# Attention and output projection of the first 128 tokens in another order

## The chip, the cores and the metric

The program runs on one NeuronCore of one Trainium2 chip. The metric is the device time of one execution in microseconds. TensorE (PE) does matmuls, PEld is its weight loading, VectorE (DVE), ScalarE (ACT) and GpSimd (POOL) do elementwise work, and SyncE (SP) issues most DMAs. Each engine runs its own instructions in order, and semaphores order the engines against each other.

## The reference

Two transformer blocks run over 256 tokens of 1024 features, in float32. Cut to what matters here, the first block is:

```python
qa, ka, va, pb, qm = split(rms_norm(x) @ w_in)
out_a = sliding_window_attention(qa, ka, va)   # 6 heads, window 128, query blocks of 128
out_b = rwkv7_mixer(token_shift(pb))           # 6 heads, state of 64x64, recurrence over tokens
out_m = memory_attention(qm, mk, mv)           # 4 heads over 256 memory tokens
x = x + concat([out_a, out_b, out_m]) @ w_out  # 1024 x 1024
x = x + conv_ffn(rms_norm(x))                  # w_up 1024 x 5632, w_down 2816 x 1024
```

The second block begins with `mod = silu(c) @ w_ada + b_ada`, which depends on c alone and whose sums are computed beside the first block. Then come two kinds of attention and a mixture of 32 experts, whose weights (about 200 MB) are streamed.

## The kernel before

The tokens are two halves of 128, called h or blk. Weights come through slots of SBUF in chunks of 2 MB. SyncE issues the chunks in one order and waits ahead of each until the slot's former chunk is used up. The instruction order of every engine is written out by hand in its own block (lines 2864 to 3135), and the PSUM banks are handed on by `take` and `free` (line 455).

The recurrence is computed in two blocks of 128 tokens as small matmuls (`rwkv_pe`, line 1316). It is a generator of 47 steps: products of the two blocks, six levels of a triangular inverse, then the state and the outputs. Its last steps are: outputs of the second block (step 44), two empty steps, and `turn(1)` (step 47), which transposes the normalised outputs so that VectorE can scale, shift and gate them (`gate(1)`, which raises `r_n` to 8). The same for the first block (`turn(0)`, `gate(0)`, `r_n` at 4) comes at step 43. The result lies in `cat`, features by tokens: tiles 0 to 2 window attention, 3 to 5 recurrence, 6 and 7 memory attention.

`weave` (line 1750) puts one step of the generator `beside_pe` (line 1678) behind each step of the recurrence, and the same is done on ScalarE and VectorE. Beside it lie 14 steps of projections, and then 36 attention steps g. Attention is worked in ten units, each two heads of one kind for one half of the tokens. Unit u computes its scores at g = 3u into banks 0 and 1, its softmax at g = 3u to 3u + 2 on VectorE and ScalarE, its transposes at 3u + 4 and its values at 3u + 5; ScalarE then copies them to `cat` and raises `a1_c`. A memory unit has 256 keys. A window unit has 128 keys in half 0 and 256 in half 1, and it adds a bias and a sink. The last unit's values fall on g = 32, beside step 47.

Behind the attention steps stand `adasum_pe(4)` and `(5)`: ones times the partial sums of ada chunks 4 and 5, which VectorE adds into a gate (`adagate_ve`, line 929). Behind these comes `wout_pe(q, 0)`, the output projection of half 0: 2 column blocks of 512 by 8 feature tiles, each product 128x128 by 128x512. `wout_pe(q, 1)` follows, with the transposes of half 0 for the feed-forward (`feat_pe`) after its first column block.

On VectorE the order behind `gate(1)` is: the two gate adds, the sums of ada chunk 6 (`ada_ve(6)`, eight instructions), half 0's first residual add (`wout_ve`), the sums of chunk 7, half 0's second add, the norm of half 0, split 0 (a weight tile cut into two parts), half 0's features, split 1, both adds of half 1, the norm and the features of half 1. The feed-forward's first product (`up_pe`) waits for `nlo` at 4, the features of both halves.

Of the kernel before, what the change touches and what calls it, by code (L numbers as in the profile page):

```python
# [87 lines left out]
END = object()  # L88
# [43 lines left out]
def block_kernel(nc, A, out):  # L132
# [13 lines left out]
    with ctx:  # L146
        s = {n: ctx.enter_context(nc.semaphore("s_" + n)) for n in SEMS}
# [6 lines left out]
        def v(ap, n):  # L154
            return ap.rearrange("p (n t) -> p n t", n=n)
# [5 lines left out]
        psum = [psum_all[:, 512 * i:512 * i + 512] for i in range(8)]  # L161
# [204 lines left out]
        chunks, held, counts = {}, {}, [0] * 10  # L366
# [45 lines left out]
        order = [(e_, z) for e_ in range(NE - 2) for z in range(3)] + [(NE - 2, 0), (NE - 2, 1), (NE - 1, 0), (NE - 1, 1), (NE - 2, 2)]  # L412
# [10 lines left out]
        for c in range(6):  # L423
            k = 4 if c < 5 else 2
            w = chunks["down", c].ap[:, 0:1024 * k].rearrange("p (k n) -> p k n", k=k)
            halves += [(("down", c), w[:, :, 512 * z:512 * z + 512]) for z in range(2)] if c < 5 else [(("down", c), w)]
        for name, k in [(("in2", i), 8) for i in range(10)] + [(("pm", 0), 4), (("pd", 0), 4)] + [(("out2", i), 8) for i in range(2)]:
            n = 4096 // k
# [23 lines left out]
        free = {b: [] for b in range(8)}  # L452
        kv, ka, kp_ = Count(), Count(), Count()

        def take(q, b):
            for w in free[b]:
                q.wait_ge(*w)
            return psum[b]

        def mm(q, o, l, r, start=True, stop=True):  # L460
            return q.eng.matmul(o, l, r, start=start, stop=stop, skip_group_check=True)  # L461
# [329 lines left out]
        def ksum_pe(q):  # L791
            hsum_pe(q, 1, 2, [sqb[0][:, 256:512], sqb[1][:, 0:256], sqb[1][:, 256:512]], "hs", (s["qk_sb"], 12))
# [140 lines left out]
            q.eng.tensor_tensor(g, psum[b], g, ADD).then_inc(s["ada"], 1)  # L933


        UNITS = [("mem", pr, blk) for pr in range(2) for blk in range(2)] + [("win", pr, blk) for pr in range(3) for blk in range(2)]
        NA = len(UNITS)
        A1_STEPS = 3 * NA + 6
        catv = v(cat, 8)
# [3 lines left out]
        def steps(of):  # L943
            n = [0]
            for kind, *_ in UNITS:
                n.append(n[-1] + of[kind])
# [5 lines left out]
        def hrow(ap, h):  # L952
            return ap[64 * (h % 2):64 * (h % 2) + 64, :]

        def unit1_at(g):
            return g // 3 if g >= 0 and g % 3 == 0 and g // 3 < NA else None

        def unit1_of(u):
            kind, pr, blk = UNITS[u]
            nk = 2 if kind == "mem" else 1 + blk  # L960
            return kind, pr, blk, nk, 128 * nk, v(P_[u % 3][:, 0:256 * nk], 2), st1[u % 3]

        def attn_pe(q, g):
            u = unit1_at(g - 4)
            if u is not None:
                kind, pr, blk, nk, w, P, st = unit1_of(u)
                q.wait_ge(s["a1_n"], A1N[u + 1])
                take(q, 2)
                for h in range(2):
                    for n in range(nk):  # L970
                        t = q.eng.transpose(psum[2][:, 128 * (nk * h + n):128 * (nk * h + n) + 128], P[:, h, 128 * n:128 * n + 128], ident)
                t.then_inc(s["a1_tr"], 1)
                free[2] = [(s["a1_pt"], u + 1)]
            u = unit1_at(g)
            if u is not None:
                kind, pr, blk, nk, w, P, st = unit1_of(u)
                if kind == "mem":
                    qt, ks = qkv[:, pr, :], [hrow(qkv[:, 6 + pr, :], h) for h in range(2)]
                else:
                    qt, ks = qkv[:, 2 + pr, :], [hrow(qkv[:, 5, :] if (2 * pr + h) // 3 == h else kb, h) for h in range(2)]  # L980
                    q.wait_ge(s["kb"], 2)
                q.wait_ge(s["qn"], 3)
                q.wait_ge(s["qk_sb"], 12)
                take(q, 0)
                take(q, 1)
                for h in range(2):
                    t = mm(q, psum[h][:, 0:w], hrow(qt, h)[:, 128 * blk:128 * blk + 128], ks[h][:, 0:w])
                t.then_inc(s["a1_sc"], 1)
                free[0] = free[1] = [(s["a1_e"], A1E[u + 1])]
            u = unit1_at(g - 5)  # L990
            if u is not None:
                kind, pr, blk, nk, w, P, st = unit1_of(u)
                q.wait_ge(s["a1_pt"], u + 1)
                q.wait_ge(s["sv_sb"], 2)
                take(q, 3)
                for h in range(2):
                    for n in range(nk):
                        if kind == "mem":
                            vs = vmv[:, n, 64 * (2 * pr + h):64 * (2 * pr + h) + 64]
                        else:  # L1000
                            vs = vav[:, n, 64 * ((2 * pr + h) // 3):64 * ((2 * pr + h) // 3) + 64]
                        t = mm(q, psum[3][64 * h:64 * h + 64, 0:128], vs, PT_[u % 2][:, 128 * (nk * h + n):128 * (nk * h + n) + 128], n == 0, n == nk - 1)
                t.then_inc(s["a1_o"], 1)
                free[3] = [(s["a1_c"], u + 1)]
# [646 lines left out]
            yield  # L1651


        def wout_pe(q, h):
            if h == 0:
                q.wait_ge(s["a1_c"], NA)
            q.wait_ge(s["r_n"], 4 * h + 4)
            for c in range(2):
                w = v(chunks["out", c].ap, 8)
                q.wait_ge(*chunks["out", c].tok)  # L1660
                b = 2 * h + c
                take(q, b)
                for k in range(8):
                    t = mm(q, psum[b], catv[:, k, 128 * h:128 * h + 128], w[:, k, :], k == 0, k == 7)
                    if k % 4 == 3 and k < 7:
                        yield
                t.then_inc(s["wo_mm"], 1)
                free[b] = [(s["x1"], b + 1)]
                yield

        def wout_ve(q, h, cs=(0, 1)):
            for c in cs:
                o = x[:, h, 512 * c:512 * c + 512]
                q.wait_ge(s["wo_mm"], 2 * h + c + 1)
                q.eng.tensor_tensor(o, psum[2 * h + c], o, ADD).then_inc(s["x1"], 1)


        def beside_pe(q):
            yield from qpair_pe(q, 2)
            yield from qpair_pe(q, 3)  # L1680
            rq_pe(q, 1)
            rq_pe(q, 2)
            ksum_pe(q)
            yield
            yield from vm_pe(q)
            kspread_pe(q)
            yield
            for g in range(A1_STEPS):
                attn_pe(q, g)
                yield  # L1690
            for i in (4, 5):
                adasum_pe(q, i, take(q, i - 2))
                free[i - 2] = [(s["ada"], i - 3)]
                yield
            yield
            yield from wout_pe(q, 0)

        def beside_sc(q):
            for _ in range(4):
# [1376 lines left out]
        @block.tensor  # L3076
        def _(e):
            q = Queue(e)
            q.wait_ge(s["cst"], 16)
            q.wait_ge(s["par"], N_GAIN)  # L3080
            par_pe(q, 0, 6)
            feat_pe(q, 0, Xn, lambda i: (s["ht1"], i + 1))
            q.wait_ge(s["ht1"], 4)
            rpair_pe(q, 0)
            q.wait_ge(s["par1"], N_PAR)
            par_pe(q, 1, 7)
            feat_pe(q, 1, Xn, lambda i: (s["ht1"], i + 5))
            rpair_pe(q, 1)
            q.wait_ge(s["par2"], N_PAR2)
            par_pe(q, 2, 5)  # L3090
            par_pe(q, 3, 6)
            q.wait_ge(s["cst2"], 32)
            bias_pe(q)
            lora_pe(q, 0)
            rpair_pe(q, 2)
            lora_pe(q, 1)
            lora_pe(q, 2)
            for _ in qpair_pe(q, 0):
                pass
            hsum_pe(q, 0, HSB, [bsv[:, i, :] for i in range(3)], "hs", (s["r_kk"], 2))  # L3100
            rpair_pe(q, 3)
            rq_pe(q, 0)
            kk_pe(q)
            rpair_pe(q, 4)
            band_pe(q)
            va_pe(q)
            for _ in qpair_pe(q, 1):
                pass
            bsum_pe(q)
            turn_pe(q)  # L3110
            weave(rwkv_pe(q), beside_pe(q))
            ft2 = (lambda i: (s["ft2"], i + 1))
            for n, _ in enumerate(wout_pe(q, 1)):
                if n == 1:
                    feat_pe(q, 2, xn1, ft2, hs=(0,))
            take(q, 7)
            for i in range(4):
                adasum_pe(q, i, psum[7][:, 4 * i:4 * i + 4])
            feat_pe(q, 2, xn1, ft2, hs=(1,))
            adapair_pe(q, 6, psum[7][:, 16:24])  # L3120
            free[7] = [(s["ada"], 4)]
            up_pe(q)
            down_pe(q, lambda: feat_pe(q, 3, xn2, ft3, hs=(0,)))
            proj2_pe(q)
            mix_pe(q)
            out2_pe(q)
            router_pe(q)
            moe_pe(q, chunks, True)
            rounds(q, lambda w: moe_pe(w, again, False), 2)
# [25 lines left out]
```

## Time and profile before

| | before |
|---|---|
| median of 3 runs | 1099.6 us (1099.22 to 1101.18) |
| profiled execution | 1100.53 us, span 1098.7 us |
| granted TensorE clock, mean | 0.932 |
| TensorE matmul busy | 916.8 us (83%) |
| VectorE busy | 540.7 us (49%) |
| ScalarE busy | 347.0 us (32%) |
| DMA | 316.69 MB, mean 288 GB/s |

Busy shares are averages over the whole span. The chain that ended last counts 52% TensorE and 30% DMA; which of them sets the pace differs by stage, and the page's 40 slices show where. Times in the timelines count from the start of the span. A line number can be that of a helper: nearly all matmuls have L461, so one tells them by their tiles (`ps<-w,cat` is the output projection). A float32 product appears as two matmul records. The granted clock is a share of 2.4 GHz.

### The profile page before, as it was taken

To read this page: it belongs to the slowest core of one execution; us is meant where nothing else is said; L and a number is where in the kernel's file an instruction comes from. 1 tells how busy PE (TensorE), PEld (TensorE's weight loads), DVE (VectorE), ACT (ScalarE), POOL (GpSimd) and SP (SyncE) were. 2 spreads that over 40 slices of the span, in tenths; PEclk is the share of its full clock that TensorE was granted. 3 is DMA by queue.
4 is the path that set the end of the run, shared out by engine and by line. 5 is a ranking of instruction groups with operands and counts; after the bars stand their busy time and mean duration, and the time that the engine had idled before them with its cause. 6 is when DMAs were issued, how large, how long until landed. Compare 5 with 4: busy or idle time off the path is not lost.

```text
span 1098.7 us, 19063 instructions
## 1 busy us (share of the span) xinstructions
PE 916.8 (83%) x8306; PEld 706.2 (64%) x8306; DVE 540.7 (49%) x1004; ACT 347.0 (32%) x678; POOL 78.7 (7%) x113
## 2 busy tenths in 40 slices
PE   5998999999999999999999988665667665667665
PEld 5786777579999887998889965332434333334332
DVE  4446668756888865698866743121212121211121
ACT  3421144236776634555563341010101000000001
POOL 3102711000000000132001000000000000000000
PEclk9898999989999999999999999888888787988888
DMA  9342484474463565796445989999999999999994
GB/s 334 128 164 86 144 299 145 158 232 157 154 210 127 180 241 196 236 288 186 142 152 199 429 350 421 431 429 428 428 429 428 429 428 429 429 429 429 427 430 169
DMA packets 76089, 316.69 MB, mean 288 GB/s; under 512 B 3983, under 2 KB 27824, under 8 KB 63456
## 3 DMA queue, kind: packets, MB, share of 16 engines
q1 hardware_dynamic: 71236, 302.24, 70.0%
q0 software_dynamic: 4624, 13.14, 4.0%
q8 instruction: 67, 1.10, 0.4%
q14 instruction: 22, 0.18, 0.0%
q10 hardware_dynamic: 140, 0.04, 0.0%
HBM read 312.24 MB, written 1.06 MB: 285 GB/s over the span
## 4 chain that ended last, share of the span: by engine, by line
PE 52%; DMA 30%; DVE 9%; ACT 3%; issue 2%; POOL 2%; SPq 1%; DVEq 0%; ACTq 0%
PE ps L461 50%; DMA w<-in_w_up 19%; DMA w<-in_w_gate 6%; DVE sp L1787 2%; DMA w<-in_w_down 2%; DMA w<-in_w_ada 2%; DMA xmem<-in_mem 1%; POOL w L833 1%; POOL w L836 1%; DVE w L902 1%; DMA rot<-q 1%; PE ps L546 0%; DVE rot L2148 0%; DVE q L2149 0%; PE ps L2600 0%
## 5 line engine op out<-in xcount | busy, mean ns | idle before, releaser
L461 PE MATMUL ps<-w,xg 128*32 128x256 f32 x2048 | 159.8, 476 | 107.5 <-DMA w<-in_w_up 83.2
L461 PE MATMUL ps<-hb,sp 128*128 128x256 f32 x1824 | 226.6, 285 | 0.0
L461 PEld LDWEIGHTS ps<-hb,sp 128*128 128x128 f32 x1824 | 220.8, 190 | 3.9 <-issue 3.0
L461 PEld LDWEIGHTS ps<-w,xg 128*32 128x32 f32 x2048 | 86.2, 133 | 180.0 <-issue 156.1
L1787 DVE TENSOR_TENSOR sp<-w,sp 128x1024 fp32r<-128x1024 f32 x122 | 144.3, 1220 | 39.6 <-ACT sp L1778 39.6
L1778 ACT ACTIVATE sp<-w 128x1024 fp32r<-128x1024 f32 x122 | 122.2, 1051 | 45.5 <-PE ps L461 43.4
L2759 DVE TENSOR_TENSOR cst<-ps,cst 64x256 f32<-64x256 f32 x32 | 13.7, 428 | 227.9 <-ACT cst L2691 227.9
L2691 ACT ACTIVATE cst<-ps 64x256 f32<-64x256 f32 x32 | 12.1, 377 | 329.8 <-PE ps L461 329.8
L2774 DVE TENSOR_TENSOR ost<-ps,cst 32x256 f32<-32x256 f32 x120 | 50.5, 421 | 101.4 <-PE ps L461 98.6
L461 PE MATMUL ps<-w,hts 128*32 128x256 f32 x1024 | 63.4, 388 | 13.8 <-ACT hts L2695 11.4
L461 PE MATMUL ps<-ht,w 128*128 128x256 f32 x256 | 62.4, 403 | 1.2 <-DMA w<-in_w_in 1.2
L461 PE MATMUL ps<-sp,ab 128*128 128x512 f32 x264 | 61.7, 395 | 0.0
L461 PEld LDWEIGHTS ps<-ht,w 128*128 128x128 f32 x256 | 50.6, 201 | 12.5 <-issue 3.1
L461 PEld LDWEIGHTS ps<-sp,ab 128*128 128x128 f32 x264 | 49.6, 188 | 11.4
L461 PEld LDWEIGHTS ps<-w,hts 128*32 128x32 f32 x1024 | 30.5, 111 | 35.3 <-ACT hts L2695 15.6
L461 PEld LDWEIGHTS ps<-pl,x 128*128 128x128 f32 x256 | 30.2, 191 | 11.5 <-DVE cst L2759 5.9
L461 PE MATMUL ps<-pl,x 128*128 128x128 f32 x256 | 33.9, 284 | 4.3 <-DVE cst L2759 3.8
L461 PE MATMUL ps<-sp,hb 128*128 128x256 f32 x192 | 26.9, 295 | 3.8 <-DVE hb L1815 2.0
L864 DVE SCALAR_TENSOR_TENSOR acc<-w,cpad,acc 128x512 f32<-128x512 f32 x30 | 29.4, 980 | 0.5
L461 PE MATMUL ps<-ost,pwt 128*128 128x512 f32 (+1 forms) x64 | 28.9, 594 | 0.0
L461 PEld LDWEIGHTS ps<-sp,hb 128*128 128x128 f32 x192 | 24.6, 196 | 6.1 <-DVE hb L1815 2.3
L461 PE MATMUL ps<-w,cat 128*128 128x512 f32 x64 | 27.8, 592 | 0.0
(398 smaller groups left out, 1146.8 us busy)
## 6 DMA issues: line engine op xcount, KB each, us to landing
w<-in_w_down SPq DMA_DIRECT2D x36, 2048.0 KB, 35.7
w<-in_w_gate SPq DMA_DIRECT2D x32, 2048.0 KB, 28.0
w<-in_w_up SPq DMA_DIRECT2D x32, 2048.0 KB, 32.3
w<-in_w_in SPq DMA_DIRECT2D x14, 2048.0 KB, 10.3
w<-in_w_up SPq DMA_DIRECT2D x22, 1024.0 KB, 7.7
w<-in_w_ada SPq DMA_DIRECT2D x8, 2048.0 KB, 9.7
w<-in_w_out SPq DMA_DIRECT2D x4, 2048.0 KB, 9.0
w<-in_w_ada POOLq DMA_DIRECT2D x8, 768.0 KB, 5.5
```

The source lines that it names most:

```text
L461: return q.eng.matmul(o, l, r, start=start, stop=stop, skip_group_check=True)
L833: e.tensor_tensor(w[:, k, :], w[:, k, :], bc(cpv[:, k, 0:1], [128, 512]), MUL).then_inc(s["ada_k"], 1)
L836: e.tensor_tensor(w[:, k, :], w[:, k, :], w[:, k + 1, :], ADD).then_inc(s["ada_k"], 1)
L864: e.scalar_tensor_tensor(out=a, in0=w[:, k, :], scalar=cpv[:, k, 0:1], in1=a, op0=MUL, op1=ADD).then_inc(s["ada_d"], 1)
L902: q.eng.scalar_tensor_tensor(out=o, in0=w[:, k - a, :], scalar=cpv[:, k, 0:1], in1=o, op0=MUL, op1=ADD).then_inc(s["ada_d"], 1)
L1778: q.eng.activation(half_w(j)[0][:, ks, :], src[:, ks, :], ACT.Copy).then_inc(s["hi"], 1)
L1787: q.eng.tensor_tensor(w[1][:, ks, :], src[:, ks, :], w[0][:, ks, :].bitcast(F), SUB).then_inc(s["split"], 1)
L2691: e.activation(sgl[i], psum[4 + e_ % 2][0:64, 0:256], ACT.Silu).then_inc(s["m_sg"], 1)
L2759: e.tensor_tensor(hh[i], psum[4 + e_ % 2][64:128, 0:256], sgl[i], MUL).then_inc(s["m_hh"], 1)
L2774: e.tensor_tensor(ost[g % 2][r:r + 32, 256 * j:256 * j + 256], psum[7][32 * j:32 * j + 32, 0:256], gq2[32 * j:32 * j + 32, :], MUL).then_i ...
```

## The change

Three things change. The list of units goes half by half, with memory units ahead of window units in each half, instead of alternating between halves. The output projection works the tiles of attention (6, 7, 0, 1, 2) ahead of those of the recurrence (3, 4, 5): for half 0 over both column blocks, for half 1 within each column block. It yields after each product and waits for the recurrence only ahead of tile 3. Half 0's projection is started beside the attention steps from g = 29 on, as `OUT_AHEAD` says, one more product is issued after each of the two adasums, and the rest behind them. In half 1's projection the transposes of half 0 come after twelve products instead of eight.

```diff
-        UNITS = [("mem", pr, blk) for pr in range(2) for blk in range(2)] + [("win", pr, blk) for pr in range(3) for blk in range(2)]
+        UNITS = [(kind, pr, blk) for blk in range(2) for kind, n in (("mem", 2), ("win", 3)) for pr in range(n)]
...
+        ATTENDED, RECURRENT = (6, 7, 0, 1, 2), (3, 4, 5)
+
         def wout_pe(q, h):
             if h == 0:
-                q.wait_ge(s["a1_c"], NA)
-            q.wait_ge(s["r_n"], 4 * h + 4)
-            for c in range(2):
-                w = v(chunks["out", c].ap, 8)
-                q.wait_ge(*chunks["out", c].tok)
+                order = [(c, k) for ks in (ATTENDED, RECURRENT) for c in range(2) for k in ks]
+            else:
+                order = [(c, k) for c in range(2) for k in ATTENDED + RECURRENT]
+            q.wait_ge(s["a1_c"], NA // 2 * (h + 1))
+            for c, k in order:
                 b = 2 * h + c
-                take(q, b)
-                for k in range(8):
-                    t = mm(q, psum[b], catv[:, k, 128 * h:128 * h + 128], w[:, k, :], k == 0, k == 7)
-                    if k % 4 == 3 and k < 7:
-                        yield
-                t.then_inc(s["wo_mm"], 1)
-                free[b] = [(s["x1"], b + 1)]
+                if k == ATTENDED[0]:
+                    q.wait_ge(*chunks["out", c].tok)
+                    take(q, b)
+                if k == RECURRENT[0]:
+                    q.wait_ge(s["r_n"], 4 * h + 4)
+                t = mm(q, psum[b], catv[:, k, 128 * h:128 * h + 128], v(chunks["out", c].ap, 8)[:, k, :], k == ATTENDED[0], k == RECURRENT[-1])
+                if k == RECURRENT[-1]:
+                    t.then_inc(s["wo_mm"], 1)
+                    free[b] = [(s["x1"], b + 1)]
                 yield
...
+        OUT_AHEAD = (0, 1, 2, 2, 2, 1, 1, 1)
...
+            first_half = wout_pe(q, 0)
             for g in range(A1_STEPS):
                 attn_pe(q, g)
+                for _ in range(OUT_AHEAD[max(g - 28, 0)]):
+                    next(first_half, END)
                 yield
             for i in (4, 5):
                 adasum_pe(q, i, take(q, i - 2))
                 free[i - 2] = [(s["ada"], i - 3)]
+                next(first_half, END)
                 yield
             yield
-            yield from wout_pe(q, 0)
+            yield from first_half
...
             for n, _ in enumerate(wout_pe(q, 1)):
-                if n == 1:
+                if n == 11:
                     feat_pe(q, 2, xn1, ft2, hs=(0,))
```

## Rows read from the trace of the kernel before

**Rows 1.** the page's 40 slices of 27.5 us: busy tenths of TensorE and of the DMA engines.

```profile
PE   5998999999999999999999988665667665667665
...
DMA  9342484474463565796445989999999999999994
```

**Rows 2.** chain of waits from 240 on: start, us, what.

```profile
239.97 181.74 PE ps L461 x1290
```

**Rows 3.** timeline of TensorE, 198 to 246: start, us, engine, line, operation [idle before].

```profile
199.33 0.65 PE L971 MATMUL ps<-cst,pr 128*128 128x128 f32 x4 [0.97 <-DVE pr L1041]
...
201.06 0.67 PE L1489 MATMUL ps<-cst,yn 128*128 128x128 f32 x3 [1.07 <-DVE yn L1582]
...
202.71 2.98 PE L461 MATMUL ps<-acc,cst 128*128 128x512 f32 x4
...
205.53 20.76 PE L461 MATMUL ps<-w,cat 128*128 128x512 f32 x48
...
226.13 1.04 PE L546 MATMUL ps<-cst,xn 128*128 128x128 f32 x8
...
233.88 3.63 PE L461 MATMUL ps<-cst,acc 128*128 128x1 f32 x32
...
237.41 1.10 PE L546 MATMUL ps<-cst,xn 128*128 128x128 f32 x8
...
238.34 2.90 PE L461 MATMUL ps<-cst,acc 128*128 128x1 f32 x16
...
241.11 5.15 PE L461 MATMUL ps<-hb,sp 128*128 128x256 f32 x24
```

**Rows 4.** timeline of VectorE, 204 to 235.

```profile
204.82 0.69 DVE L933 TENSOR_TENSOR g1b<-ps,g1b 128x512 f32<-128x512 f32 x1 [1.60 <-PE ps L461]
...
205.73 0.69 DVE L933 TENSOR_TENSOR g1b<-ps,g1b 128x512 f32<-128x512 f32 x1 [0.22 <-PE ps L461]
...
219.47 0.69 DVE L1675 TENSOR_TENSOR x<-ps,x 128x512 f32<-128x512 f32 x1
...
221.99 0.75 DVE L534 TENSOR_SCALAR xn<-x,small 128x1024 f32<-128x1024 f32 x1 [0.27 <-ACT small L514]
...
222.94 2.36 DVE L1787 TENSOR_TENSOR sp<-w,sp 128x1024 fp32r<-128x1024 f32 x2 [0.19 <-ACT sp L1778]
...
226.77 1.29 DVE L557 TENSOR_TENSOR ht<-ps,par 128x512 f32<-128x512 f32 x2 [1.47 <-PE ps L546]
...
229.70 2.36 DVE L1787 TENSOR_TENSOR sp<-w,sp 128x1024 fp32r<-128x1024 f32 x2 [0.25 <-ACT sp L1778]
...
234.07 0.69 DVE L1675 TENSOR_TENSOR x<-ps,x 128x512 f32<-128x512 f32 x1 [1.41 <-PE ps L461]
```

**Rows 5.** window of VectorE alone, 205.7 to 220.2.

```profile
205.70:220.20 14.50, 13.93 (x19) 1.00 0.78 272
```

**Rows 6.** windows A:B: us, busy per engine (instructions), granted clock (PEclk), DMA.

```profile
201.30:204.80 3.50, 3.50 (x14) 1.85 (x13) 1.43 (x4) 0.28 (x1) 0.00 (x0) 0.51 0.20 16
238.90:245.70 6.80, 6.80 (x33) 6.80 (x33) 4.43 (x8) 3.05 (x4) 0.00 (x0) 0.50 1.10 350
```

**Rows 7.** window over the recurrence's levels.

```profile
145.80:170.50 24.70, 24.70 (x545) 20.95 (x546) 20.87 (x42) 12.03 (x32) 3.56 (x6) 0.93 0.55 199
```

**Rows 8.** timeline of TensorE: its waits between 170 and 198.

```profile
173.74 0.88 PE L461 MATMUL ps<-xz,moff 64*64 64x64 f32 x12 [1.00 <-ACT xz L1535]
...
178.45 0.91 PE L461 MATMUL ps<-xz,t 64*64 64x64 f32 x12 [0.55 <-DVE t L1626]
...
190.69 1.55 PE L461 MATMUL ps<-rhs,zf 128*128 128x64 f32 x12 [0.51 <-ACT rhs L1552]
```

**Rows 9.** timeline of SyncE's queue: w_out, and the last chunk of w_ada.

```profile
155.84 16.69 SPq L2897 DMA_DIRECT2D w<-in_w_out  x2
...
203.25 0.37 SPq L2897 DMA_DIRECT2D w<-in_w_ada  x1
```

**Rows 10.** the page's DMA issues: KB each, median us from issue to landing.

```profile
w<-in_w_ada SPq DMA_DIRECT2D x8, 2048.0 KB, 9.7
```


## The prediction

> **What bounds the kernel now.** I read the page's slices first [rows 1]. TensorE is nearly full up to slice 23 while the DMA engines are half used; from slice 23 on (604 us) the DMA engines are full, streaming the second block's expert weights. Every early transfer of that stream waits for a slot that TensorE's progress frees, so a shift of TensorE in the first 600 us should reach the end one for one. The chain of waits supports it: from 239.97 on one piece of TensorE lasts 181.74 us, the feed-forward's first product [rows 2]. So what the change is worth is read off one moment, the first feed-forward matmul, which starts at 241.11 [rows 3].
>
> Next the timeline of TensorE from the end of the recurrence to there [rows 3]. It waits 0.97 us for the last attention unit's probabilities and 1.07 us for the normalised output of the recurrence; then it is busy without a gap: adasum of chunks 4 and 5 (2.98 us), the output projection of half 0 and of half 1's first column (the 48 passes in 20.76 us: 0.4325 us a pass, two passes a product, so 0.865 us a product), transposes of half 0, half 1's second column, adasum of 0 to 3, transposes of half 1, adapair.
>
> Then the timeline of VectorE over the same stretch [rows 4], which shows the second limit. It waits 1.60 us for adasum 4 and 0.22 us for adasum 5. From 205.73, when it adds adasum 5 into the gate, until 220.16 (219.47 plus 0.69) it never rests: 13.93 us busy in 14.5 [rows 5]. This is the gate, the sums of ada chunk 6, half 0's first residual add, the sums of chunk 7, the second add. Half 0's norm, split 0, half 0's features, split 1, and half 1's two adds follow, with only two waits for TensorE, of 1.47 us and 1.41 us. VectorE's queue, begun by adasum 5, is thus within 3 us of being the bound.
>
> **The change part by part.**
>
> (a) *Products put ahead.* The recurrence has 47 steps and attention step g stands beside step g + 15, so OUT_AHEAD places 1, 2 and 2 products behind the other work of attention steps 29, 30 and 31, all ahead of the last turn, which stands at the start of step 47; 2 more follow the last unit's values (g = 32), 3 the empty steps 33 to 35. One comes behind adasum 4, one behind adasum 5, and 4 remain: 16, the same number as before. Nothing is computed twice. All 16 were behind both adasums; now 10 are ahead of adasum 4 and one stands between the two.
>
> What TensorE gains: the waits of 0.97 and 1.07 us go (2.04 us), since five products of 0.865 us (4.3 us) lie there. The granted clock was 0.51 from 201.3 to 204.8 [rows 6], the 1.2 GHz level, right after these two waits: 3.5 us at half rate cost 1.7 us of work. I take both as gained, 3.7 us; the bounds for the clock term are 0 and 1.7.
> The Trainium skill (TensorE: Matmul & The Clock Gate, "HAM oscillation — how this bites in real kernels") holds that gaps between matmuls throttle the engine and that a loop arranged without them keeps it warm. The trace agrees as far as the fall to 0.51 goes; by that rule the whole 1.7 us comes back.
>
> What VectorE gets: a new start. TensorE is free at 198.36 (199.33 less 0.97). From there to the end of adasum 5 now stand 3 products (2.60), 4 transposes (0.65), 2 products (1.73), the turn (0.67), the last unit's values (0.65, estimated like the 4 transposes), 5 products (4.33), adasum 4 (0.87, priced like a product, since both are 128x512), a product (0.87) and adasum 5 (0.87): 13.2 us, so 211.6. Before it was 205.7. The gate add of chunk 5 begins 5.9 us later, and everything queued behind it on VectorE begins later by the same.
> The Trainium skill (same page, "Architectural detail") says that ScalarE and VectorE are strict FIFO. The trace agrees: chunk 6's sums, which need nothing of TensorE, start only behind the two gate adds. Were it otherwise, chunk 6 would be done during the wait and the sum would come out as in rival P.
>
> What is late next: both adds of half 0 are through at 220.16 + 5.9 = 226.1. Norm: 2.6 us (220.16 to 222.74), so 228.7. TensorE has by then finished half 0 (211.6 + 5 x 0.865 = 215.9) and the twelve products of half 1 ahead of feat_pe (10.4 us: 226.3), and stands still for 2.4 us. It makes the transposes at 228.7, but VectorE is in split 0 (2.36 us plus 0.19) until 231.3, so its features, which started at 226.77, start at 231.3: plus 4.5, because the wait of 1.47 us was absorbed. The next stretch keeps its length up to half 1's first add; the 1.41 us before the second add goes too, as TensorE is through with half 1 at about 233.2 (transposes 1.0 and four products 3.5). Left over: 5.9 - 1.47 - 1.41 = 3.0 us. Half 1's norm, transposes, adapair and the first feed-forward matmul follow as before: 3.0 us later.
>
> (b) *feat_pe at n == 11 instead of 1.* Four more products ahead of it, 3.5 us. Nothing, because the normalised half arrives after that place (226.3 against 228.7). With that cover gone it would cost up to 3.5 us of delay to the transposes.
>
> (c) *Order of the units.* Same ten units, so the same work in total. Near the cheap units of half 0 (128 keys) TensorE has less to do beside the recurrence's levels, while later steps get dearer units. In the levels it is busy 24.70 of 24.70 us and VectorE 20.87 [rows 7]; later it waits 1.00, 0.55 and 0.51 us [rows 8]. At best these 2.06 us vanish. At worst as much idle time appears in the levels where VectorE becomes the slower one: -2.1 to +2.1 us. I take -0.4: the wait of 0.55 us is the nearest row, as VectorE had a masked window unit ahead of it where now stands a memory unit without bias and sink, and the others wait on ScalarE's order, which hardly changes.
>
> (d) *Waits of the output projection.* At g = 29 it asks for five units instead of ten (done at step 17), for the w_out chunks, issued from 155.84 with the second at 172.5 [rows 9] and landed long before 198, and for banks 0 and 1, which the last unit's exponentials release before the probabilities of 199.33 can exist. Nothing. Chunk 7 of w_ada is issued at 203.25 when recurrence and attention are both done; that moves to about 206, plus 9.7 us [rows 10] is 216, and VectorE wants it at about 219. Covered by 3 us, else one for one. The first w_up chunk waits for chunk 6's sums and is issued about 6 us later, at 218; split 0 reads it at 228. Covered as well.
>
> (e) *Clock at the end.* The granted clock is 0.50 from 238.9 to 245.7 [rows 6], after the one-column matmuls of adasum; 4.6 us of that lie in the feed-forward. New gaps of 2.4 us (before half 0's transposes) and about 3.8 us (before half 1's) make it no better: between 0 and 1.7 us more, of which I take 0.2, as the low stretch was there already.
>
> Sum: 3.0 - 0.4 + 0.2 = +2.8 us. The profiled execution took 1100.53 us (span 1098.7); with the change 1103.3. The median of the runs shown is 0.9 lower, 1099.6, so the forecast is 1102.4.
>
> **Rivals.**
> *P, TensorE alone sets the pace.* If VectorE's queue had slack that I don't see, the feed-forward would start earlier by what TensorE gained: 3.7 plus 0.4, 1095.5. For it: TensorE has no gap from 201.06 to 241.11 in the trace. Against it: VectorE rests only 2.9 us between 205.73 and 234.76, and 5.9 is more. 0.12.
> *O, the order gives it back.* The waits of (c) all go, adasum 5 comes 2.1 us sooner, and 5.9 shrinks to 3.8: the start moves by 3.8 - 2.9 = +0.9, with the clock 1.1: 1100.7. For it: three waits in one stretch of chained steps. Against it: two of them hang on ScalarE. 0.25.
> *C, the clock falls in the new gap.* It drops in the 2.4 us before half 0's transposes, stays low through the sparse matmuls, and the feed-forward runs some 3.4 us longer at 1.2 GHz, losing 1.7 instead of 0.2: 1103.9. For it: gaps of 0.97 and 1.07 us were enough at 201. Against it: the low stretch before 245.7 exists anyway. 0.13.
> By the Trainium skill's section named in (a) the new gaps would speak for C.
> *The forecast*, VectorE's delayed queue: 0.50.
>
> **How the numbers follow.** A measurement of this kernel tells about 0.2%, 2.2 us, from no change: the lines are 1097.4 and 1101.8. Faster by more is P and a remainder, 0.14. Within is O and a fifth of the forecast's cases (+2.8 has an own range of +1.5 to +4): 0.31. Slower by more: 0.55. The range leaves P out at the lower end and takes in O and C: 1098.6 to 1104.6.
>
> **What would show it.** Right: products of w and cat run from about 198 without a gap, at full clock through 206; VectorE waits some 4 us for adasum 4 and its chunk 6 sums start near 212; TensorE waits 2 to 3 us ahead of half 0's transposes and about 4 us ahead of half 1's; the first feed-forward matmul at 243.5 to 244, and the expert stream later by as much. Wrong: a feed-forward start before 241, chunk 6's sums before 210, or a difference that arises past 250.

## The result and the profile after

| | before | after |
|---|---|---|
| median | 1099.68 us (18 runs) | 1106.26 us (18 runs) |
| ratio of the runs, 95% interval | | 1.0051, 1.0030 to 1.0072 |
| profiled execution | 1100.53 us, span 1098.7 | 1105.69 us, span 1103.9 |
| granted clock, mean | 0.932 | 0.926 |

The change makes the kernel slower by 0.51% (+5.6 us by the ratio). The direction was forecast; the size was 2.8 us, and the median, 1106.26 us, lies above the range of 1098.6 to 1104.6. Disturbed runs are left out of the ratios; the profiled execution of one experiment (u_rhs) was such a run, so its trace is not read.

TensorE after, from the last solve of the recurrence (solve 1, `ps<-rhs,zf`) to the feed-forward's first matmul; it answers to [rows 3]:

```profile
187.40 1.74 PE L461 MATMUL ps<-rhs,zf 128*128 128x64 f32 x12 [0.72 <-ACT rhs L1552]
...
201.02 5.15 PE L461 MATMUL ps<-w,cat 128*128 128x512 f32 x6
...
208.16 0.49 PE L1489 MATMUL ps<-cst,yn 128*128 128x128 f32 x3
...
215.28 1.02 PE L461 MATMUL ps<-acc,cst 128*128 128x512 f32 x2
...
216.14 14.76 PE L461 MATMUL ps<-w,cat 128*128 128x512 f32 x34
...
233.25 1.97 PE L546 MATMUL ps<-cst,xn 128*128 128x128 f32 x8 [2.35 <-DVE xn L534]
...
239.15 3.63 PE L461 MATMUL ps<-cst,acc 128*128 128x1 f32 x32
...
244.79 1.97 PE L546 MATMUL ps<-cst,xn 128*128 128x128 f32 x8 [2.02 <-DVE xn L534]
...
246.56 3.41 PE L461 MATMUL ps<-cst,acc 128*128 128x1 f32 x16
...
249.83 0.56 PE L461 MATMUL ps<-hb,sp 128*128 128x256 f32 x1
```

VectorE after, which answers to [rows 4]:

```profile
214.63 0.69 DVE L933 TENSOR_TENSOR g1b<-ps,g1b 128x512 f32<-128x512 f32 x1 [4.48 <-PE ps L461]
...
216.34 0.69 DVE L933 TENSOR_TENSOR g1b<-ps,g1b 128x512 f32<-128x512 f32 x1 [1.02 <-PE ps L461]
...
229.92 0.68 DVE L1679 TENSOR_TENSOR x<-ps,x 128x512 f32<-128x512 f32 x1
...
232.44 0.75 DVE L534 TENSOR_SCALAR xn<-x,small 128x1024 f32<-128x1024 f32 x1 [0.27 <-ACT small L514]
...
233.38 2.36 DVE L1797 TENSOR_TENSOR sp<-w,sp 128x1024 fp32r<-128x1024 f32 x2 [0.19 <-ACT sp L1788]
...
235.66 1.28 DVE L557 TENSOR_TENSOR ht<-ps,par 128x512 f32<-128x512 f32 x2
...
240.87 1.28 DVE L1679 TENSOR_TENSOR x<-ps,x 128x512 f32<-128x512 f32 x2
```

Windows over three stretches of the kernel after (us, busy of PE, PEld, DVE, ACT, POOL, granted clock, DMA), against [rows 6]:

```profile
188.70:205.20 16.50, 16.50 (x63) 12.51 (x63) 6.12 (x16) 7.59 (x16) 0.00 (x0) 0.50 0.04 14
232.50:236.20 3.70, 2.95 (x10) 2.44 (x11) 3.51 (x4) 1.80 (x2) 0.00 (x0) 0.57 1.10 351
245.00:253.30 8.30, 8.30 (x40) 8.30 (x40) 5.32 (x9) 3.15 (x4) 0.14 (x2) 0.50 1.03 327
```

The reader is to see two things. First, the queue of the prediction: adasum 5 is issued at 215.28, the second gate add starts at 216.34 instead of 205.73, half 0's second add at 229.92 instead of 219.47, TensorE waits 2.35 us for half 0's norm, and VectorE's two waits of [rows 4], 1.47 and 1.41 us, are gone. Second, something the prediction did not have: the first six passes `w,cat` take 5.15 us (0.86 us each, twice the 0.4325 of [rows 3]), because the granted clock was 0.50 from 188.7 to 205.2, the 1.2 GHz level, while TensorE was busy 16.50 of 16.50 us. Before, it was 0.51 for 3.5 us in this stage.

From solve 1 to the feed-forward's first matmul it took 50.4 us before (190.69 [rows 8] to 241.11 [rows 3]), and takes 249.83 - 187.40 = 62.4 after, 12.0 more. Solve 1 itself begins 3.3 us sooner than in the profile before, so the feed-forward starts 8.7 us later. What became of this is in the chain of waits, first before, then after:

```profile
495.99 5.68 PE ps L461 x48
...
1013.43 1.98 PE ps L461 x32
```

```profile
502.85 5.69 PE ps L461 x48
...
1018.80 1.98 PE ps L461 x32
```

The same piece of the second block starts 6.9 us later, the same piece near the end 5.4 us later (the span: 5.2).

### The profile page after: what moved, and what is told of

It is laid out like the page before. It is cut to its first block, busy times and chain, and to the rows that moved or that the text cites. A ratio compares the mean times of both kernels' runs of the same rounds, so it can differ in the third digit from the quotient of the medians.

```text
span 1103.9 us, 19062 instructions
## 1 busy us (share of the span) xinstructions
PE 920.1 (83%) x8306; PEld 708.7 (64%) x8306; DVE 540.2 (49%) x1004; ACT 347.0 (31%) x678; POOL 77.3 (7%) x113
## 3 DMA queue, kind: packets, MB, share of 16 engines
HBM read 312.24 MB, written 1.06 MB: 284 GB/s over the span
## 4 chain that ended last, share of the span: by engine, by line
PE 56%; DMA 28%; DVE 9%; ACT 4%; issue 2%; POOL 1%; SPq 0%; POOLq 0%; ACTq 0%; DVEq 0%
PE ps L461 54%; DMA w<-in_w_up 21%; DMA w<-in_w_gate 3%; DVE sp L1797 2%; DMA w<-in_w_down 2%; DMA w<-in_w_in 1%; DVE w L864 1%; DMA rot<-q 1%; ACT sp L1788 1%; PE ps L2610 0%; PE ps L971 0%; PE ps L546 0%; ACT hts L2705 0%; ACT sd L2110 0%; DVE acc L864 0%
## 5 line engine op out<-in xcount | busy, mean ns | idle before, releaser
L2784 DVE TENSOR_TENSOR ost<-ps,cst 32x256 f32<-32x256 f32 x120 | 50.5, 420 | 100.1 <-PE ps L461 97.3
L461 PE MATMUL ps<-w,cat 128*128 128x512 f32 x64 | 31.7, 647 | 0.0
```

The costliest lines, as they stand in the source:

```text
L2784: e.tensor_tensor(ost[g % 2][r:r + 32, 256 * j:256 * j + 256], psum[7][32 * j:32 * j + 32, 0:256], gq2[32 * j:32 * j + 32, :], MUL).then_i ...
```

## The experiments

One measure serves for all profiles: **S, the time from the start of solve 1 to the start of the feed-forward's first matmul**. It leaves out scatter from before solve 1. "Ratio" is the time against the kernel before on the same chip.

| kernel | order of units | gap ahead of solve 1 | long low clock near 190 | S, us | ratio (95% interval) |
|---|---|---|---|---|---|
| before | old | 0.51 | no | 50.4 | 1 |
| b_again | old | 0.51 | no | 50.5 | |
| gap1 | old | 0.60 | no | 50.3 | 0.9985 (0.9961 to 1.0009) |
| gap2 | old | 0.69 | no | 50.4 | 0.9985 (0.9961 to 1.0009) |
| gap3 | old | 0.78 | yes | 57.3 | 1.0020 (0.9991 to 1.0048) |
| gap6 | old | 1.06 | yes | 56.7 | 1.0039 (1.0022 to 1.0056) |
| b_rhs | old | none | no | 50.6 | 0.9998 (0.9977 to 1.0020) |
| u_only | new | 0.72 | yes | 59.4 | 1.0049 (1.0020 to 1.0078) |
| u_rhs1 | new | 0.50 | no | 50.5 | 0.9986 (0.9961 to 1.0010) |
| u_rhs | new | | | | 0.9980 (0.9956 to 1.0005) |
| after | new | 0.72 | yes | 62.4 | 1.0051 (1.0030 to 1.0072) |
| a_again | new | 0.72 | yes | 62.4 | 1.0076 (1.0042 to 1.0109) |
| w_only | old | 0.51 | no | 54.6 | 1.0021 (0.9997 to 1.0045) |
| v_first | new | 0.72 | yes | 58.1 | 1.0019 (0.9989 to 1.0049) |
| a_rhs | new | none | no | 54.6 | 1.0037 (1.0017 to 1.0057) |
| av_rhs | new | none | no | 50.3 | 0.9984 (0.9966 to 1.0002) |
| best | new | none | no | 48.4 | 0.9952 (0.9931 to 0.9973) |

Two theories stood at the start. V: VectorE's queue waits behind adasum 5, as predicted. C: the clock falls near 190, for a cause then unknown. The fences below show, for each kernel, solve 1 in TensorE's timeline with the wait ahead of it, and a window from 2.5 to 8.5 us behind its start, whose granted clock stands third from the end.

**a_again**: the changed kernel, unedited.

> The changed kernel as it is, once more, with a new profile. Theory V (VectorE's queue is put behind adasum 5) expects of every profile that the second gate add starts 5 to 6 us later than before whatever the clock does, and the feed-forward's first matmul about 3 us later. Theory C (the granted clock at the recurrence's last steps falls, and stays low until the dense products run) expects the low stretch of the first profile (188.7 to 205.2, 16.5 us at 0.50) to return, and without it only theory V's 3 us to be left. If the stretch is chance, this profile lacks it and the ratio to before comes down to about 1.003; if it belongs to the new order, it returns and the ratio is 1.005 to 1.006.

```profile
189.31 1.96 PE L461 MATMUL ps<-rhs,zf 128*128 128x64 f32 x12 [0.72 <-ACT rhs L1552]
```

```profile
191.80:197.80 6.00, 6.00 (x27) 4.96 (x26) 2.02 (x4) 2.98 (x4) 0.00 (x0) 0.50 0.00 0
```

The stretch came back (190.3 to 207.3), and S is 62.4 again. It is not the chance of one profile.

**u_only**: the kernel before with `UNITS` of the change, nothing else.

```diff
-        UNITS = [("mem", pr, blk) for pr in range(2) for blk in range(2)] + [("win", pr, blk) for pr in range(3) for blk in range(2)]
+        UNITS = [(kind, pr, blk) for blk in range(2) for kind, n in (("mem", 2), ("win", 3)) for pr in range(n)]
```

> The kernel before with the new order of the ten units alone; the output projection stays behind both adasums. Theory V expects no loss: 1.000, within 0.2%, with adasum 5 done where before had it or up to 2 us sooner. Theory C, if the low clock comes from the order of the units (dear units at the end, beside the small matmuls of the state), expects the clock to fall here too near 190 and the time to be +2 to +4 us. In the changed kernel solve 1 began 3.3 us sooner than before (187.4 against 190.7); if that is the order's doing it is seen here as well.

```profile
187.94 1.57 PE L461 MATMUL ps<-rhs,zf 128*128 128x64 f32 x12 [0.72 <-ACT rhs L1552]
```

```profile
190.40:196.40 6.00, 6.00 (x27) 4.90 (x26) 2.32 (x6) 2.81 (x5) 0.00 (x0) 0.50 0.01 2
```

The order of the units alone brings the low clock and 0.49%. Theory V, which expected 1.000 here, does not explain the whole of the loss.

**w_only**: the change with the old order of units.

```diff
-            q.wait_ge(s["a1_c"], NA // 2 * (h + 1))
+            q.wait_ge(s["a1_c"], NA - 1 + h)
```

> The changed kernel with the old order of units; half 0's projection waits for nine units instead of five, since the ninth is half 0's last. Theory V expects +3 us against before, as in the changed kernel, since 11 products stand ahead of adasum 5 all the same. Theory C with the order of units as its cause expects no low stretch near 190 and the +3 us alone; with the products as its cause, a low stretch as in the changed kernel, +5 to +6 us.

```profile
189.43 1.55 PE L461 MATMUL ps<-rhs,zf 128*128 128x64 f32 x12 [0.51 <-ACT rhs L1552]
```

```profile
191.90:197.90 6.00, 5.55 (x42) 4.42 (x42) 4.54 (x12) 5.29 (x14) 0.00 (x0) 1.00 0.02 5
```

No long stretch, and S longer by 4.2 us. So the products ahead of the adasums and the order of the units each cost by themselves: 4.2 and 9.0 us of S (w_only and u_only), against 12.0 together. The ratio, 1.0021, is nearer to +2.3 us than to the +3 expected, but its interval holds both.

**v_first**: the changed kernel, with VectorE's chunk 6 ahead of the gate adds.

```diff
-            yield
-            for i in (4, 5):
-                adagate_ve(q, i, i - 2, i - 3)
-                yield
...
                 for _ in ada_ve(q, i):
                     pass
+                if i == 6:
+                    for j in (4, 5):
+                        adagate_ve(q, j, j - 2, j - 3)
                 wout_ve(q, 0, (i - 6,))
```

> The changed kernel with one thing moved on VectorE: the sums of ada chunk 6 go ahead of the two gate adds, so they run while TensorE is at the products and adasums. Theory V expects the 6.2 us of these sums to disappear from the queue behind adasum 5: half 0's second add and all behind it some 5 to 6 us sooner than in the changed kernel, the feed-forward's first matmul 3 to 5 us sooner, and the time 3 to 5 us under the changed kernel's, at or below before (0.998 to 1.001 of before). A rival by which only the clock matters expects it to stay at the changed kernel's time, within 1 us.

VectorE's timeline: the sums of chunk 6, both gate adds, half 0's second add.

```profile
210.32 4.69 DVE L864 SCALAR_TENSOR_TENSOR w<-w,cpad 128x512 f32<-128x512 f32 x6
...
215.98 1.27 DVE L933 TENSOR_TENSOR g1b<-ps,g1b 128x512 f32<-128x512 f32 x2
...
224.59 0.68 DVE L1679 TENSOR_TENSOR x<-ps,x 128x512 f32<-128x512 f32 x1
```

The sums run at 210.32, ahead of the gate adds, and the second add comes at 224.59 instead of 229.92. S falls by 4.3 us and the time by about 4 us, from 1105 or 1106 to 1101.4, though the clock stays low near 190. Theory V holds for its part. The ratio, 1.0019, is just above the 0.998 to 1.001 expected, which had reckoned nothing for the clock, and its interval (0.9989 to 1.0049) overlaps that of the changed kernel (from 1.0030).

**gap2, gap1.** What in the new order touches the clock? ScalarE's timeline ahead of solve 1, first before, then after:

```profile
189.37 0.37 ACT L1058 ACTIVATE pr<-ps,small 128x128 f32<-128x128 f32 x1
...
190.09 0.55 ACT L1552 ACTIVATE rhs<-ps 128x192 f32<-128x192 f32 x2
```

```profile
185.98 0.48 ACT L1058 ACTIVATE pr<-ps,small 128x256 f32<-128x256 f32 x1
...
186.80 0.55 ACT L1552 ACTIVATE rhs<-ps 128x192 f32<-128x192 f32 x2
```

The ninth unit is a half 0 unit before (128 keys, 0.36 us an exponential) and a half 1 unit after (256 keys, 0.48 us). Its two exponentials stand ahead of the copies of solve 1's right-hand side (L1552), so the gap grows from 0.51 to 0.72 us. The two kernels lengthen the gap in the old order:

```diff
             yield
+            for i in range(2):
+                e.activation(sml(112 + i, 1), ones[:, 0:1], ACT.Exp)
             q.wait_ge(s["r_mm"], RN["rhs1",])
```

> The kernel before, with two small ScalarE instructions of one column added ahead of the copies of the right-hand side (L1552); their results are not used. They delay solve 1, so TensorE's gap ahead of it grows from 0.51 us to about 0.85. Theory C (a longer gap ahead of solve 1 lets the granted clock fall, and the small matmuls behind it keep it low until the dense products come) expects a stretch at 0.50 from about 191 to 206 and +3 to +6 us. The rival, that the fall belongs to the dearer units of the new order and not to the gap, expects the profile of before with everything 0.4 us later: +0.4 us.

> The same with one such instruction: the gap ahead of solve 1 becomes about 0.7 us, as in the changed kernel (0.72). Theory C expects the low stretch in the profile, perhaps not in every run, and +2 to +5 us; its rival +0.2 us and no stretch.

The kernel gap2:

```profile
191.29 1.55 PE L461 MATMUL ps<-rhs,zf 128*128 128x64 f32 x12 [0.69 <-ACT rhs L1554]
```

```profile
193.80:199.80 6.00, 5.10 (x41) 4.08 (x40) 4.57 (x13) 5.29 (x14) 0.00 (x0) 1.00 0.02 8
```

Each instruction added only 0.09 us, so the gaps were 0.60 and 0.69 us, not the 0.7 and 0.85 expected. Neither lost the clock nor time. This went against theory C as first put, and left open whether the dearer units were needed.

**u_rhs, a_rhs**: the new order, without the gap. Both copies go to VectorE, in the kernel with the order alone and in the changed kernel.

```diff
-            q.wait_ge(s["r_mm"], RN["rhs1",])
-            for z in range(2):
-                e.activation(rhs_b[:, 192 * z:192 * z + 192], psum[7 - z][:, 0:192], ACT.Copy).then_inc(s["r_rhs"], 1)
...
+            q.wait_ge(s["r_mm"], RN["rhs1",])
+            for z in range(2):
+                e.tensor_copy(rhs_b[:, 192 * z:192 * z + 192], psum[7 - z][:, 0:192]).then_inc(s["r_rhs"], 1)
             spread_of(0)
```

> The kernel before with the new order of units alone, and with both copies of the right-hand side (L1552) moved from ScalarE to VectorE, which is idle there. The gap of 0.72 us ahead of solve 1 should shrink to about 0.1 to 0.3. Theory C expects no low stretch between 188 and 200 (a short one at 201 as in before may stay), and 4 to 6 us less than u_only: 0.998 to 1.001 of before. The rival (the new order's matmul mix is what lets the clock fall) expects the stretch to stay and the time at u_only's, about 1.005.

> The changed kernel with both copies of the right-hand side moved to VectorE. Theory C expects no low stretch near 190, adasum 5 done near 209 instead of 216 to 218, and with it what theory V alone predicts: 1.001 to 1.003 of before, 3 to 6 us under the changed kernel. The rival expects the changed kernel's time less 0.5 us.

TensorE in a_rhs: solve 1, adasum 5, the transposes of half 0 and of half 1, the feed-forward.

```profile
188.96 1.55 PE L461 MATMUL ps<-rhs,zf 128*128 128x64 f32 x12
...
208.96 1.02 PE L461 MATMUL ps<-acc,cst 128*128 128x512 f32 x2
...
226.91 1.09 PE L546 MATMUL ps<-cst,xn 128*128 128x128 f32 x8 [2.34 <-DVE xn L534]
...
238.52 1.97 PE L546 MATMUL ps<-cst,xn 128*128 128x128 f32 x8 [3.62 <-DVE xn L534]
...
243.56 2.69 PE L461 MATMUL ps<-hb,sp 128*128 128x256 f32 x11
```

VectorE in a_rhs: the gate add of chunk 5, both adds of half 1.

```profile
210.02 0.69 DVE L933 TENSOR_TENSOR g1b<-ps,g1b 128x512 f32<-128x512 f32 x1 [1.02 <-PE ps L461]
...
234.60 1.28 DVE L1679 TENSOR_TENSOR x<-ps,x 128x512 f32<-128x512 f32 x2
```

Solve 1 follows without a gap and the low stretch is gone: adasum 5 comes 20.0 us behind solve 1, against 27.9 after. S is 54.6, the same as w_only's, which is theory V alone. The time followed less well: 1.0037 lies above the 1.001 to 1.003 expected, and is only 1.5 us under the result's 1.0051 and 4.3 us under a_again's 1.0076, with intervals that overlap, where S fell by 7.8 us. The clearer pair is u_rhs and u_only: 0.9980 against 1.0049, 0.7% less, with intervals that lie apart. With u_rhs's trace not read, that the order alone keeps its clock without the long gap is seen in u_rhs1 below.

**gap6, b_rhs.**

> The kernel before with six unused one-column ScalarE instructions ahead of the copies of the right-hand side. One of them widened the gap ahead of solve 1 by 0.09 us, two by 0.18 (0.51 to 0.60 to 0.69), so six give about 1.05 us, more than the changed kernel's 0.72. If the length of the gap alone decides (theory C as first put), the granted clock falls behind it and stays at 0.50 until about 206: +4 to +6 us. If the dearer mix of the new order is needed as well (fewer and smaller matmuls with the gap among them), the old order keeps its clock and the time is before's plus 0.5 us.

```profile
190.37 2.83 PE L461 MATMUL ps<-rhs,zf 128*128 128x64 f32 x12 [1.06 <-ACT rhs L1554]
```

```profile
192.90:198.90 6.00, 6.00 (x28) 5.23 (x28) 1.22 (x3) 3.47 (x5) 0.00 (x0) 0.50 0.01 4
```

A gap of 1.06 us in the old order does what the changed order does: clock 0.50, S +6.3 us, 0.39% (gap6 is gap2 with six instructions).

> The kernel before with both copies of the right-hand side on VectorE: the gap of 0.51 us goes in the old order of units, where no low stretch stood near 190. Expected: the recurrence ends 0.4 us sooner, the same short low stretch at 201 to 205, and 0 to -0.6 us (0.999 to 1.0005 of before). If this gains as much as it did in the new order (0.7%), the moved copies do something else than keep the clock up.

b_rhs, the same copies moved in the old order, gains nothing (0.9998, S 50.6). In these pairs the moved copies repay only where the clock would have fallen.

**gap3, u_rhs1, b_again**, for what was still open: length or mix. gap3 is gap2 with three instructions; u_rhs1 is u_rhs with only one of the copies moved.

> The kernel before with three unused one-column ScalarE instructions ahead of the copies of the right-hand side: a gap of about 0.78 us ahead of solve 1, between the 0.69 of gap2 (clock kept) and the 1.06 of gap6 (clock lost), and just over the 0.72 of the new order of units (clock lost in four profiles of four). If the length of the gap decides alone, with its edge at about 0.7 us, the clock falls near 190 and the time is +3 to +5 us. If the old order bears a gap of this length, it keeps its clock, +0.3 us, and the new order's dearer units beside the recurrence count as well.

```profile
192.81 1.55 PE L461 MATMUL ps<-rhs,zf 128*128 128x64 f32 x12 [0.78 <-ACT rhs L1554]
```

```profile
195.30:201.30 6.00, 6.00 (x27) 4.80 (x27) 3.53 (x9) 4.21 (x11) 0.00 (x0) 0.52 0.01 4
```

> The new order of units alone with one of the two copies on VectorE and the other left on ScalarE: the gap shrinks from 0.72 to about 0.45 us, less than the old order's 0.51. If the gap's length decides, the clock is kept and the time is that of u_rhs, 0.997 to 1.000 of before; if the new order's mix decides, it falls near 190 as in u_only, 1.004 to 1.006.

```profile
188.58 1.55 PE L461 MATMUL ps<-rhs,zf 128*128 128x64 f32 x12 [0.50 <-ACT rhs L1552]
```

```profile
191.10:197.10 6.00, 5.53 (x47) 4.52 (x46) 4.58 (x13) 5.36 (x14) 0.00 (x0) 1.00 0.02 5
```

> The kernel before once more for a second profile. Both theories expect a gap of 0.51 us ahead of solve 1, full clock from 186 to 200, and the short low stretch behind the waits of 0.97 and 1.07 us. A long low stretch here would say that the fall near 190 is chance.

```profile
193.26 1.55 PE L461 MATMUL ps<-rhs,zf 128*128 128x64 f32 x12 [0.51 <-ACT rhs L1552]
```

```profile
195.80:201.80 6.00, 5.07 (x41) 4.06 (x39) 4.60 (x13) 5.29 (x14) 0.00 (x0) 1.00 0.02 5
```

The old order loses its clock at 0.78 us, and the new order keeps it at 0.50. The length of the gap decides at this place, and not the mix of the order: the edge lies between 0.69 and 0.78 us in the old order and between 0.50 and 0.72 us in the new one. At the edge it is probably not the same in each run. Of gap3's ten times that the ratio uses, four are 1097.7 to 1099.3 us with a mean granted clock of 0.931 to 0.935, and six are 1103.0 to 1106.8 us with 0.922 to 0.929, so that its interval still touches no change; the trace is that of one of the six. The kernel before had about 0.2 us to spare.

**av_rhs, best**: both repairs, and a version built on them. av_rhs is a_rhs with v_first's order on VectorE. best puts the adasums ahead of the last eleven products and half 0's transposes behind four products of half 1. On VectorE chunk 7 goes behind half 0's features, ahead of split 0, and split 1 behind half 1's features; ScalarE's order follows (left out here):

```diff
                 attn_pe(q, g)
+                if g == 32:
+                    for i in (4, 5):
+                        adasum_pe(q, i, take(q, i - 2))
+                        free[i - 2] = [(s["ada"], i - 3)]
...
-                if n == 11:
+                if n == 3:
...
-            for i in (6, 7):
-                for _ in ada_ve(q, i):
-                    pass
-                wout_ve(q, 0, (i - 6,))
+            for _ in ada_ve(q, 6):
+                pass
+            for i in (4, 5):
+                adagate_ve(q, i, i - 2, i - 3)
+            wout_ve(q, 0)
             norm_ve(q, 2, x, xn1, hs=(0,))
+            feat_ve(q, 2, ht2, col("ffn_norm_g", 0, 8), "ft2", hb, (0,))
+            for _ in ada_ve(q, 7):
+                pass
             split_ve(q, 0)
-            feat_ve(q, 2, ht2, col("ffn_norm_g", 0, 8), "ft2", hb, (0,))
-            split_ve(q, 1)
             wout_ve(q, 1)
...
             feat_ve(q, 2, ht2, col("ffn_norm_g", 0, 8), "ft2", hb, (1,))
+            split_ve(q, 1)
```

> The changed kernel with both repairs: the copies on VectorE (clock) and chunk 6's sums ahead of the gate adds (VectorE's queue). Theory C and theory V together expect no low stretch near 190, half 0's second add at about 218 instead of 230, the feed-forward's first matmul at 238.5 to 240, and 4 to 5 us under a_rhs: 0.998 to 1.000 of before. If V is wrong it stays at a_rhs's 1.0037.

TensorE in av_rhs:

```profile
187.16 1.55 PE L461 MATMUL ps<-rhs,zf 128*128 128x64 f32 x12
...
237.42 8.82 PE L461 MATMUL ps<-hb,sp 128*128 128x256 f32 x50
```

> The changed kernel with the copies on VectorE, both adasums right behind the last unit's values and ahead of the remaining eleven products, and VectorE's order: chunk 6's sums, gate adds, both adds of half 0, its norm and features, then chunk 7's sums, split 0, half 1's adds, norm and features, split 1; transposes of half 0 after four products of half 1. By theory V half 0's norm no longer waits for chunk 7, TensorE never stands still for it, and the feed-forward starts at 237 to 238.5: 3 to 4 us under before, 0.996 to 0.998, provided the clock does not fall. If it falls at half 1's gap as before, up to 2 us of that are lost.

TensorE in best: solve 1, the adasums, half 0's transposes, the feed-forward.

```profile
187.81 1.55 PE L461 MATMUL ps<-rhs,zf 128*128 128x64 f32 x12
...
201.71 1.98 PE L461 MATMUL ps<-acc,cst 128*128 128x512 f32 x4
...
216.51 1.10 PE L546 MATMUL ps<-cst,xn 128*128 128x128 f32 x8
...
236.18 10.09 PE L461 MATMUL ps<-hb,sp 128*128 128x256 f32 x68
```

In av_rhs S is 50.3, back at before's, and the time is at or just under before's: the two causes make up the whole loss. In best half 0's transposes come at 216.51 and the feed-forward at 236.18, both sooner than expected (237 to 238.5 for the latter). It takes 0.9952 of before's time (0.9931 to 0.9973), -5.3 us, and beats both kernels. Of that S shows 2.0 us; the rest was not traced to a place.

## Why the prediction was right or wrong

**(a), VectorE's new start: right.** 5.9 us later was the working. a_rhs has the change with the clock at full rate, as assumed: the gate add of chunk 5 starts at 210.02, 21.1 us behind solve 1, against 15.0 before: +6.0. TensorE's wait of 2.4 us ahead of half 0's transposes measured 2.34 us there. The left-over behind the two absorbed waits (3.0 us) can be read at half 1's second add: it ends 46.9 us behind solve 1 instead of 44.1, +2.8. The feed-forward started at 243.56, in the span given (243.5 to 244), but that is partly luck: solve 1 began 1.7 us sooner in a_rhs than in the profile before. Counted from solve 1 the feed-forward is 4.2 us later, which is these 2.8 us and the 1.3 of (e) below.

**(a), the clock: wrong; this is the failed step.** "I take both as gained, 3.7 us; the bounds for the clock term are 0 and 1.7." The waits of 0.97 and 1.07 us did go. But the bounds had no loss in them: the clock fell for 16.5 us and more at an earlier place, which the products could not protect, since they begin only behind it. Its price: adasum 5 comes 27.9 us behind solve 1 after and 20.0 in a_rhs, 7.9 us. With the clock kept, a_rhs's ratio puts the time at 1103.7 us, inside the range; with it lost, the median is 1106.3, outside. The interval of a_rhs reaches into that of the result, so this last step rests on S and on the pair u_only and u_rhs more than on these two times.

**(c), the order of the units: here the clock was lost.** The failed sentence is the one on two of the three waits: "the others wait on ScalarE's order, which hardly changes". The order stays, the lengths do not: two exponentials grow by 0.12 us each. The wait of 0.51 us was counted as at most 0.51 us to gain; it grew to 0.72, and 0.2 us of waiting cost nearly 8 us. The wait of 0.55 us, which the forecast took as gained, did go in the profile after, and that of 1.00 us became 0.79; but both lie ahead of solve 1, where the profiles scatter more than that (gap1, in the old order, has solve 1 at 187.66). What the order does to the work itself stays small: without the clock's fall it measured 0.9980 and 0.9986 in u_rhs and u_rhs1, against 0.9998 in b_rhs; a gain of 0 to 2 us (-0.4 was taken), not told apart from none.

**(e), the clock at the end: mis-sized, inside its bounds.** 0.2 us was taken of 0 to 1.7. In a_rhs the stretch from half 1's second add to the feed-forward lasts 7.7 us (235.88 to 243.56) instead of 6.3 (before: 234.76 to 241.11): +1.3, with the transposes at 1.97 us instead of 1.10 and adapair at 3.41 instead of 2.90.

**(b) and (d): right.** TensorE waited for half 0's norm in spite of the four products more. Chunk 7 was issued at 210.17, later than the 206 reckoned, and VectorE took it up at 223.74 without a wait.

**Rivals.** P is out: with S 4.2 us longer in a_rhs and back at 50.3 in av_rhs, where only VectorE's order differs, VectorE's queue is the bound. The 2.9 us of rest held against P are VectorE's waits for TensorE alone; it was busy 23.58 us from 205.73 to 234.76, so it rested 5.45 in all, the other 2.6 mostly behind ScalarE in the norm and the splits. O is not what happened: of its three waits one went, one shrank and the third grew. C had the right means, a fall of the clock behind a gap, and its +4.3 us was nearer to the result than the forecast, but it named another place. At that gap, of 2.35 us, the clock did fall in the profile after, for 3.4 us, and not in a_again: hidden either way behind VectorE, as S is 62.4 in both. C's dearer end did come, in the main, as (e).
The Trainium skill (TensorE: Matmul & The Clock Gate, "What's actually happening") puts it that activity releases the throttle. The trace agrees only in part: TensorE was busy throughout from 188.7, and the clock came back only behind 205.2, during the passes of 512 columns.

**Carrying to the end.** A shift was to arrive one for one. In the profile after, 8.7 us at the feed-forward became 5.2 at the end, 1.9 of it lost up to the second block and 1.7 beyond. Over runs, a_rhs gives +4.1 us for 4.2 us of S, w_only +2.3 for 4.2, gap6 +4.3 for 6.3, u_only +5.4 for 9.0, the change +5.6 for 12.0. So a shift without the long low stretch arrived whole in one kernel of two, and the dear stretch arrived by a quarter (v_first, +2.1 for 7.7) to two thirds. Part of the reason may be that the clock near 190 was not lost in every timed run. The change's sixteen times that the ratio uses lie in two groups, seven of 1100.6 to 1102.6 us with a granted clock of 0.931 in the mean, and nine of 1105.7 us or more with 0.925. An estimate: 13 us more at half rate (16.5 against 3.5) are 0.006 of a run of 1104 us, the distance of the two groups. The only two traces of the changed kernel, 1105.69 and 1109.58 us, both lost it, and gap6's times do not fall apart like this, so this stays likely and not shown. How the clock falls in later stages was not compared either.

## What to carry to other kernels

When work is reordered, look at the short waits that stay, not only at those that go: a wait of half a microsecond ahead of small matmuls can stand just short of the length at which TensorE drops to half rate there, and then the half rate lasts through the small matmuls behind it (here S grew by 6.3 to 9.0 us in gap6, gap3 and u_only). Price a moved filler by what is queued behind it on the other engines too: here eleven products put ahead of a 128x512 sum that VectorE's queue waited for. And test such causes by lengthening or removing the wait alone, with the rest left as it is.

## What the runs showed of the hardware

Ahead of solve 1 the loss of the clock went by the length of the gap. With small matmuls around it (most of 64 and 128 columns), gaps of 0.50, 0.51 (three profiles), 0.60 and 0.69 us kept 2.4 GHz, and gaps of 0.72 (four profiles), 0.78 and 1.06 us were followed by a fall to 1.2 GHz, 0 to 2.7 us behind the start of solve 1.

The length is no rule for other places. In the kernel before, the wait of 1.00 us ahead of 173.74 [rows 8] kept the clock (1.00 from 173 to 188). The gap ahead of half 0's transposes, 2.34 or 2.35 us in four profiles, kept it in a_again and a_rhs and lost it in after and w_only. What else decides was not varied.

Once low, the clock did not come back during the recurrence's matmuls, 12 to 18 us long up to the first product of 512 columns. In the profile after, in a_again and in v_first TensorE counted as busy all that time; in u_only, gap3 and gap6 one wait of 1.4 us lies in it. Matmuls of the same kind ran at 1.00 from 191 to 199 in the profile before. The clock came back 2 to 5 us behind the start of the 512-column matmuls: in after from 201.02, back at 205.7; in gap6 from 208.67, back at 210.9.

One unused one-column ScalarE instruction cost 0.09 us in a full queue (gaps of 0.51, 0.60, 0.69 and 0.78 us with none to three of them).
